# Moving the high and the low weight tiles to other places modulo 256 bytes in a one-core transformer kernel

## The chip, the cores and the metric

The kernel runs on one NeuronCore of a Trainium2 chip. The metric is the device time of one execution in microseconds (us), taken as the median of several runs. A difference of 0.2% (3.4 us) is about what a measurement of this kernel can tell from no change.

## The reference, cut to what matters

Two transformer layers follow each other on 512 tokens of width 1024, all in 32-bit floats:

```
h = LN(alpha*h + 0.5*swiglu(h))                  # ffn1, 1024 -> 2816 -> 1024
h = LN(alpha*h + mixers(h))                      # in 1024 -> 3072, out 1024 -> 1024
h = LN(alpha*h + cross_attention(h, mem))        # q, k, v, o: 1024 x 1024, 256 memory rows
h = LN(alpha*h + 0.5*swiglu(h))                  # ffn2
x = h + gate * (ga*(ya@w_a) + gb*(yb@w_b) + gc*(yc@w_c)) @ w_o
# ya: neighbourhood attention with 256 context keys, yb, yc: convolution branches; in 1024 -> 8704
```

Nearly all of the arithmetic is products of an activation matrix with a weight matrix. The change touches none of it: the same numbers are computed from the same operands.

## The kernel before, in words

**Splitting.** A 32-bit operand is split into a high part (rounded to the type fp32r, which TensorE multiplies in one pass) and a low part (what the rounding left, in fp32r as well). A product of two 32-bit matrices is then three matmuls: high weight by high activation, high weight by low activation, low weight by high activation. `product` does this (lines 417 to 423):

```
for n, (a, b) in enumerate(((wh, xh), (wh, xl), (wl, xh))):
    if moving_weights:
        a, b = b, a
    mm = nc.tensor.matmul(dst, a, b, start=start and n == 0, stop=stop and n == 2)
```

The first operand of `matmul` is the stationary one: it is loaded into the array by an LDWEIGHTS of its own, which the trace shows on the row PEld. The second, the moving one, is streamed past it. In most stages the weights are stationary, a piece of 128x128 (512 bytes in each partition), and an activation chunk of 512 tokens moves (2048 bytes in each partition; 256 tokens where the memory, the context or half of the tokens are meant). In token_strip (line 473), and in it only, the roles are exchanged: 512 columns of weights move and 128 tokens stand.

**The weight stream.** All the weights come from HBM as strips of 128x1024. SP loads each strip into one of four slots of `raw` (load, line 2201) once DVE has finished with the slot's last strip. ScalarE copies it to `w_hi` (split_hi, line 401, the instruction on line 407), VectorE writes raw minus w_hi to `w_lo` (split_lo, line 409, the instruction on line 414), and TensorE uses both (feature_strip, line 425, and its variants; the matmul itself is on line 422). ScalarE waits, before it writes a slot of w_hi, until TensorE is through with the strip that was there. Each of the three tiles has four slots.

**Stages.** ffn1 (to about 370 us, with its down projection), the token mixers (to 560), the output projection of the mixers and cross attention (to 780; the keys of the context, with ctx_hi and ctx_lo as moving tiles, near 762 to 774), ffn2 (to 1175), the neighbourhood attention and convolutions (to 1462), the merge and last projection (to 1707). The order within a stage is written out by hand on each engine, with semaphores between them.

**Where the tiles lie.** Tiles in SBUF are laid one behind the other in the order of their declaration, each rounded up to a multiple of 32 bytes, and a tile of an inner scope takes the place of those of a scope that was closed. These are the lines that matter:

```
172  raw = sb("raw", [P, RING, SB * P])            # 4 x 1024 x 4 = 16384 bytes in a partition
173  w_hi = sb("w_hi", [P, RING, SB * P], F32R)    # 16384
174  w_lo = sb("w_lo", [P, RING, SB * P], F32R)    # 16384
175  h = sb("h", [P, KD, T])                       # 16384
179  a_hi = sb("a_hi", [P, KD, T], F32R)           # 16384, a_lo the same
181  cols = sb("cols", [P, NCOLS])                 # 271 x 4 = 1084, rounded up to 1088
182  consts = sb("consts", [P, 2, P])
239  xs = sb("xs", [P, 3, 8, 2], F32, ph)          # 192
240  ctx_hi = sb("ctx_hi", [P, KD, M], F32R, ph)   # 8192, ctx_lo the same
```

Call the address of raw modulo 256 bytes r (it is 128). Since 16384 is a multiple of 256, w_hi, w_lo, h, a_hi and a_lo all begin at r too. The small tiles between a_lo and work add up to a multiple of 256, so hid_hi, hid_lo, mix_h, mix_l, side_hi, side_lo, y_hi, y_lo, m_hi, m_lo, memv_hi and xpt_hi, all the other operands of line 422, begin at r as well. Pieces within a tile are multiples of 512 bytes apart. Two kinds of tile stand elsewhere: consts and the constant matrices behind it begin at r + 64, since cols ends 64 bytes past a multiple of 256; ctx_hi and ctx_lo begin at r - 64, since xs ahead of them has 192 bytes.

Of the kernel before, what the change touches and what calls it, by code (L numbers as in the profile page):

```python
# [27 lines left out]
P = 128  # L28
# [129 lines left out]
def hybrid_blocks(nc, stream, ada_in, cond_in, x_in, mem_in, ctx_in, cols_in, const_in, mask_in, rows_in, wst_in, band_in, rpb_in,  # L158
                  out):
    with ExitStack() as ctx:  # L160
# [3 lines left out]
        def sb(name, shape, dt=F32, scope=ctx):  # L164
            return scope.enter_context(nc.sbuf_tensor(name, shape, dt))
# [4 lines left out]


        raw = sb("raw", [P, RING, SB * P])
        w_hi = sb("w_hi", [P, RING, SB * P], F32R)
        w_lo = sb("w_lo", [P, RING, SB * P], F32R)
        h = sb("h", [P, KD, T])
        with ExitStack() as ph:
            cond_row = sb("cond_row", [P, 2, D], F32, ph)
# [2568 lines left out]
```

## Time and profile before

| | us |
|---|---|
| median of 3 runs (1707.86 to 1708.67) | 1708.23 |
| span of the profiled execution, first to last instruction | 1706.6 |
| PE (matmuls) busy in it | 1691.5 |
| PEld (weight loads) busy | 1394.7 |
| DVE (VectorE) busy | 994.7 |
| ACT (ScalarE) busy | 683.6 |

The span is the only time that is recorded of the profiled execution; the median is 1.6 us above it. Busy times of different engines overlap. A matmul's recorded duration goes from its start to the end of its last result, so that successive matmuls overlap in the record; the pace of TensorE is read from the difference of two starts. The granted TensorE clock is 1.00 of full speed (2.4 GHz) in every stretch.

### The profile page before, as it was taken

How to read it: one execution, taken by the hardware profiler on the slowest of the kernel's cores; microseconds unless marked ns; L12 is line 12 of the kernel's file. 1: busy time of each engine (PE TensorE's matmuls, PEld its weight loads, DVE VectorE, ACT ScalarE, POOL GpSimd, SP SyncE). 2: the span in 40 equal slices, each digit the busy share in tenths (PEclk: the TensorE clock that was granted, in tenths of full speed). 3: DMA queues.
4: the chain of work that ended last, by engine and by line, in shares of the span. 5: the costliest groups of instructions: out<-in, count | busy, mean ns of one | idle time of the engine just before them, and what ended most of it. 6: DMA issues, size and time to landing. Idle time of an engine off the chain costs nothing.

```text
span 1706.6 us, 22901 instructions
## 1 busy us (share of the span) xinstructions
PE 1691.5 (99%) x8500; PEld 1394.7 (82%) x8500; DVE 994.7 (58%) x1341; ACT 683.6 (40%) x975; POOL 166.8 (10%) x158
## 2 busy tenths in 40 slices
PE   9999999999999999999999999999999999999999
PEld 7888888888787888888888888877778787788887
DVE  5333339987965784666333333457976869844442
ACT  4222232246454465434222223346454445732330
POOL 0000000112004521013000000013011020000000
DMA  5333247633122353223332233323333222243331
GB/s 216 98 98 98 91 138 231 222 121 119 52 98 66 109 182 137 67 82 123 98 98 94 92 130 117 109 87 118 85 99 95 86 83 86 74 123 109 104 109 62
DMA packets 51476, 188.05 MB, mean 110 GB/s; under 512 B 5776, under 2 KB 6288, under 8 KB 50512
## 3 DMA queue, kind: packets, MB, share of 16 engines
q1 hardware_dynamic: 44640, 161.50, 29.7%
q10 hardware_dynamic: 5184, 16.00, 2.9%
q0 software_dynamic: 1584, 9.60, 1.6%
q8 instruction: 47, 0.77, 0.2%
q14 instruction: 21, 0.17, 0.0%
HBM read 182.89 MB, written 4.19 MB: 110 GB/s over the span
## 4 chain that ended last, share of the span: by engine, by line
PE 89%; DVE 7%; ACT 2%; issue 1%; DMA 0%; POOL 0%; SPq 0%; DVEq 0%; ACTq 0%; POOLq 0%
PE proj L422 83%; DVE w_lo L414 1%; PE aux L1859 1%; PE aux L1846 1%; PE aux L1619 1%; PE aux L1836 1%; DVE y L2016 0%; ACT w_hi L407 0%; DVE score L1221 0%; DVE qk L1264 0%; DVE md L1242 0%; PE aux L566 0%; DVE qk L1265 0%; PE aux L1839 0%; DVE md L1241 0%
## 5 line engine op out<-in xcount | busy, mean ns | idle before, releaser
L414 DVE TENSOR_TENSOR w_lo<-raw,w_hi 128x1024 fp32r<-128x1024 f32 x300 | 380.5, 1270 | 388.8 <-ACT w_hi L407 382.0
L422 PE MATMUL proj<-a_hi,w_hi 128*128 128x512 f32 (+1 forms) x1536 | 600.8, 391 | 3.3 <-DVE a_lo L909 1.8
L422 PE MATMUL proj<-a_hi,w_lo 128*128 128x512 f32 (+1 forms) x1536 | 591.3, 385 | 0.0
L422 PE MATMUL proj<-a_lo,w_hi 128*128 128x512 f32 (+1 forms) x1536 | 591.0, 385 | 0.0
L407 ACT ACTIVATE w_hi<-raw 128x1024 fp32r<-128x1024 f32 x300 | 315.3, 1053 | 233.4 <-PE proj L422 164.3
L422 PEld LDWEIGHTS proj<-a_hi,w_hi 128*128 128x128 f32 x1536 | 288.5, 188 | 67.9 <-issue 5.8
L422 PEld LDWEIGHTS proj<-a_lo,w_hi 128*128 128x128 f32 x1536 | 288.7, 188 | 58.4 <-issue 2.9
L422 PEld LDWEIGHTS proj<-a_hi,w_lo 128*128 128x128 f32 x1536 | 288.5, 188 | 58.5
L422 PE MATMUL proj<-hid_hi,w_hi 128*128 128x512 f32 (+1 forms) x374 | 142.6, 381 | 0.0
L422 PE MATMUL proj<-hid_hi,w_lo 128*128 128x512 f32 (+1 forms) x374 | 140.9, 377 | 0.0
L422 PE MATMUL proj<-hid_lo,w_hi 128*128 128x512 f32 (+1 forms) x374 | 140.8, 377 | 0.0
L971 ACT ACTIVATE hid_hi<-work 128x512 f32 (+1 forms) x44 | 27.8, 632 | 196.5 <-DVE work L988 196.5
L988 DVE TENSOR_TENSOR work<-sq,proj 128x512 f32<-128x512 f32 x44 | 30.2, 687 | 106.7 <-PE proj L422 106.7
L2016 DVE SCALAR_TENSOR_TENSOR y<-glu,wtap,y 128x512 f32 (+1 forms) x120 | 90.6, 755 | 3.2
L422 PEld LDWEIGHTS proj<-hid_hi,w_hi 128*128 128x128 f32 x374 | 70.4, 188 | 13.9 <-issue 0.7
L422 PEld LDWEIGHTS proj<-hid_lo,w_hi 128*128 128x128 f32 x374 | 70.4, 188 | 13.6 <-issue 0.7
L422 PEld LDWEIGHTS proj<-hid_hi,w_lo 128*128 128x128 f32 x374 | 70.4, 188 | 12.9
L966 ACT ACTIVATE sq<-proj 128x512 f32<-128x512 f32 x44 | 26.3, 597 | 114.9 <-PE proj L422 114.9
L993 DVE TENSOR_TENSOR hid_lo<-work,hid_hi 128x512 f32 (+1 forms) x44 | 30.5, 693 | 39.7 <-ACT hid_hi L971 39.7
L728 POOL TENSOR_SCALAR h<-h,cols 128x512 f32<-128x512 f32 x32 | 40.7, 1275 | 98.2 <-DVE a_lo L710 50.6
L1906 ACT ACTIVATE npr<-aux,ns 128x512 f32<-128x512 f32 x32 | 22.0, 689 | 48.0 <-DVE ns L2031 48.0
L580 POOL TENSOR_TENSOR work<-h 128x512 f32<-128x512 f32 x3 | 4.7, 1574 | 364.2 <-DVE h L646 364.2
(368 smaller groups left out, 2011.1 us busy)
## 6 DMA issues: line engine op xcount, KB each, us to landing
raw<-stream SPq DMA_DIRECT2D x303, 512.0 KB, 3.5
ctxk<-ada_in ACTq DMA_DIRECT2D x12, 512.0 KB, 3.7
ctxv<-ada_in ACTq DMA_DIRECT2D x12, 512.0 KB, 3.9
out<-h ACTq DMA_DIRECT2D x7, 256.0 KB, 2.0
h<-x_in SPq DMA_DIRECT2D x3, 512.0 KB, 8.7
btab<-rpb_in POOLq DMA_DIRECT2D x4, 384.0 KB, 3.5
cond_row<-cond_in ACTq DMA_DIRECT2D x1, 1024.0 KB, 5.9
side<-mem_in POOLq DMA_DIRECT2D x1, 1024.0 KB, 5.2
```

Source lines behind the costliest of these rows:

```text
L407: nc.scalar.activation(w_hi[:, st.slot], raw[:, st.slot], ACT.Copy).then_inc(hi_ready, 1)
L414: nc.vector.tensor_tensor(w_lo[:, st.slot], raw[:, st.slot], w_hi[:, st.slot].bitcast(F32), ALU.subtract).then_inc(lo_ready, 1)
L422: mm = nc.tensor.matmul(dst, a, b, start=start and n == 0, stop=stop and n == 2)
L728: nc.gpsimd.tensor_scalar(m.dst[:, c], m.dst[:, c], 1.0, m.shift(c), ALU.mult, ALU.add).then_inc(n_raw, 1)
L966: nc.scalar.activation(sq[:, j // 2], res, ACT.Silu).then_inc(proj_read[g.slot], 1)
L971: nc.scalar.activation(hc, work[:, j // 2], ACT.Copy).then_inc(hid_h, 1)
L988: nc.vector.tensor_tensor(work[:, j // 2], sq[:, j // 2], res, ALU.mult).then_inc(proj_read[g.slot], 1)
L993: nc.vector.tensor_tensor(a, work[:, j // 2], b.bitcast(F32), ALU.subtract).then_inc(hid_l, 1)
L1619: mm = nc.tensor.matmul(aux[:, u % 2, t * M:(t + 1) * M], xq[:, 2 * hd + kk, at:at + P], memk[:, 2 * hd + kk], start=(kk == 0), stop=(kk = ...
L1836: nc.tensor.matmul(aux[:, n, :M], nq[part, at], grid(nk[part], ROWS, BAND_AT[cb], BAND), start=True, stop=True)
L1906: nc.scalar.activation(npr[:, u % 2], aux[:, u % 2], ACT.Exp, bias=ns[:, 0, u:u + 1], accum_out=ns[:, 1, u:u + 1]).then_inc(u_exp, 1)
L2016: ins = nc.vector.scalar_tensor_tensor(dst, src, wtap[:, tap:tap + 1], dst, ALU.mult, ALU.add)
```

## The change

Three unused tiles are declared between the others. w_hi moves up by 64 bytes, w_lo by 128, and h and everything behind it by 64 + 64 + 128 = 256 bytes.

```
         raw = sb("raw", [P, RING, SB * P])
+        sb("shift_hi", [P, 16])
         w_hi = sb("w_hi", [P, RING, SB * P], F32R)
+        sb("shift_lo", [P, 16])
         w_lo = sb("w_lo", [P, RING, SB * P], F32R)
+        sb("shift_behind", [P, 32])
         h = sb("h", [P, KD, T])
```

Modulo 256 bytes raw stays at r, w_hi comes to r + 64, w_lo to r + 128, and every other tile keeps its place: the activations at r, consts at r + 64, ctx_hi and ctx_lo at r - 64. No instruction, semaphore, DMA or order changes.

## Rows read from the trace of the kernel before

**Rows 1.** The page: span, busy time by engine, chain that ended last by engine and line.
```profile
span 1706.6 us, 22901 instructions
...
PE 1691.5 (99%) x8500; PEld 1394.7 (82%) x8500; DVE 994.7 (58%) x1341; ACT 683.6 (40%) x975; POOL 166.8 (10%) x158
...
PE 89%; DVE 7%; ACT 2%; issue 1%; DMA 0%; POOL 0%; SPq 0%; DVEq 0%; ACTq 0%; POOLq 0%
PE proj L422 83%; DVE w_lo L414 1%; PE aux L1859 1%; PE aux L1846 1%; PE aux L1619 1%; PE aux L1836 1%; DVE y L2016 0%; ACT w_hi L407 0%; DVE score L1221 0%; DVE qk L1264 0%; DVE md L1242 0%; PE aux L566 0%; DVE qk L1265 0%; PE aux L1839 0%; DVE md L1241 0%
```

**Rows 2.** Chain that ended last, by line, of 0:370, 370:560, 560:780, 780:1175, 1175:1462, 1462:1707 us.
```profile
by line: PE proj L422 96.6%; DMA h<-x_in 1.0%; PE aux L594 0.2%; DVE h L903 0.2%; DVE h L885 0.2%; DVE a_lo L2413 0.2%; ACT a_hi L2269 0.2%; PE aux L836 0.2%; issue 0.1%; ACT work L347 0.1%; PE aux L840 0.1%; DVE work L891 0.1%; DVE h L869 
...
by line: PE proj L422 55.4%; issue 4.6%; DVE score L1221 4.0%; DVE qk L1264 3.9%; DVE md L1242 3.6%; DVE qk L1265 3.6%; DVE md L1241 3.2%; ACT md L1269 3.0%; ACT md L1370 2.5%; PE aux L1313 1.9%; PE aux L1330 1.9%; PE aux L1322 1.8%; PE aux
...
by line: PE proj L422 59.6%; DVE w_lo L414 6.0%; PE aux L1619 4.7%; issue 2.9%; ACT w_hi L407 2.4%; DVE side L704 2.4%; DVE h L675 2.0%; DVE h L704 1.8%; DVE h L652 1.6%; DVE work L745 1.5%; DVE side_lo L710 1.4%; POOL work L736 1.4%; ACT x
...
by line: PE proj L422 95.4%; PE aux L566 1.7%; PE aux L1780 0.4%; issue 0.4%; DVE a_lo L710 0.3%; ACT L1917 0.3%; DVE w_lo L414 0.3%; PE aux L594 0.2%; PE aux L600 0.2%; PE aux L602 0.2%; PE aux L606 0.2%; PE aux L608 0.2%; DVE h L704 0.2%;
...
by line: PE proj L422 71.2%; PE aux L1859 5.7%; PE aux L1846 5.6%; PE aux L1836 3.3%; DVE y L2016 2.8%; PE aux L1839 2.3%; issue 1.6%; PE aux L1884 0.9%; PE aux L1874 0.9%; PE proj L1879 0.9%; DVE w_lo L414 0.9%; ACT L1917 0.4%; ACT L1932 0
...
by line: PE proj L422 98.0%; PE aux L546 0.4%; PE aux L562 0.4%; issue 0.2%; DVE h L2546 0.2%
```

**Rows 3.** Timeline of PE, 512-column matmuls: start us, duration us, what.
```profile
1501.00 0.39 PE L422 MATMUL proj<-a_lo,w_hi 128*128 128x512 f32 x1
1501.23 0.39 PE L422 MATMUL proj<-a_hi,w_lo 128*128 128x512 f32 x1
1501.45 0.39 PE L422 MATMUL proj<-a_hi,w_hi 128*128 128x512 f32 x1
...
1503.72 0.39 PE L422 MATMUL proj<-a_lo,w_hi 128*128 128x512 f32 x1
```

**Rows 4.** The same, 256 columns, moving tile side_hi or side_lo.
```profile
609.90 0.28 PE L422 MATMUL proj<-side_lo,w_hi 128*128 128x256 f32 x1
610.02 0.28 PE L422 MATMUL proj<-side_hi,w_lo 128*128 128x256 f32 x1
610.14 0.28 PE L422 MATMUL proj<-side_hi,w_hi 128*128 128x256 f32 x1
...
610.98 0.28 PE L422 MATMUL proj<-side_lo,w_hi 128*128 128x256 f32 x1
```

**Rows 5.** The same, 256 columns, moving tile ctx_hi or ctx_lo.
```profile
763.51 0.28 PE L422 MATMUL proj<-ctx_hi,w_hi 128*128 128x256 f32 x1
763.62 0.28 PE L422 MATMUL proj<-ctx_lo,w_hi 128*128 128x256 f32 x1
763.73 0.28 PE L422 MATMUL proj<-ctx_hi,w_lo 128*128 128x256 f32 x1
...
765.55 0.28 PE L422 MATMUL proj<-ctx_hi,w_hi 128*128 128x256 f32 x1
```

**Rows 6.** Instructions on tile side_hi: count, duration ns min/median/max, first and last start.
```profile
L422 PEld LDWEIGHTS proj<-side_hi,w_lo x64: 187/192/192, 588.9 to 617.1; 128*128 128x128 f32 x64
L422 PE MATMUL proj<-side_hi,w_lo x64: 277/283/283, 589.0 to 617.2; 128*128 128x256 f32 x64
L717 ACT ACTIVATE side_hi<-side,cols x8: 508/510/512, 582.0 to 592.9; 128x256 fp32r<-128x256 f32 x8
L710 DVE SCALAR_TENSOR_TENSOR side_lo<-side,cols,side_hi x8: 474/478/1508, 583.4 to 593.5; 128x256 fp32r<-128x256 f32 x8
```

**Rows 7.** The same for tile ctx_hi.
```profile
L422 PEld LDWEIGHTS proj<-ctx_hi,w_lo x32: 187/188/189, 762.9 to 773.5; 128*128 128x128 f32 x32
L422 PE MATMUL proj<-ctx_hi,w_lo x32: 276/276/281, 763.0 to 773.6; 128*128 128x256 f32 x32
L717 ACT ACTIVATE ctx_hi<-side,modv x8: 496/500/512, 658.2 to 673.3; 128x256 fp32r<-128x256 f32 x8
L710 DVE SCALAR_TENSOR_TENSOR ctx_lo<-side,modv,ctx_hi x8: 477/482/485, 658.7 to 673.9; 128x256 fp32r<-128x256 f32 x8
```

**Rows 8.** All of line 422: busy time and count, PE then PEld.
```profile
0.00:1707.00 1707.00, 1572.47 (x7146) 1287.11 (x7146) 1.00 0.34 110
```

**Rows 9.** Groups of line 422 with 256 columns, shapes kept apart.
```profile
L422 PE MATMUL proj<-side_hi,w_lo 128*128 128x256 f32 x64 | 18.1, 283 | 0.0
L422 PE MATMUL proj<-a_hi,w_lo 128*128 128x256 f32 x64 | 18.1, 283 | 0.0
L422 PE MATMUL proj<-hid_hi,w_lo 128*128 128x256 f32 x44 | 12.4, 283 | 0.0
```

**Rows 10.** The page: the two split instructions, ACT's and DVE's.
```profile
L414 DVE TENSOR_TENSOR w_lo<-raw,w_hi 128x1024 fp32r<-128x1024 f32 x300 | 380.5, 1270 | 388.8 <-ACT w_hi L407 382.0
L407 ACT ACTIVATE w_hi<-raw 128x1024 fp32r<-128x1024 f32 x300 | 315.3, 1053 | 233.4 <-PE proj L422 164.3
```

**Rows 11.** Instructions on tiles mv and xp, 128 columns.
```profile
L1313 PE MATMUL aux<-score,mv x32: 270/275/275, 502.8 to 508.7; 128*128 128x128 f32 x32
...
L1629 PE MATMUL aux<-consts,xp x32: 270/273/330, 686.6 to 711.7; 128*128 128x128 f32 x32
```

**Rows 12.** The page: DMA issues of the weight stream.
```profile
raw<-stream SPq DMA_DIRECT2D x303, 512.0 KB, 3.5
```

**Rows 13.** Busy us and counts in two stretches: PE, PEld, DVE, ACT, POOL; clock, DMA, GB/s.
```profile
1200.00:1300.00 100.00, 99.95 (x554) 79.33 (x553) 86.40 (x137) 50.35 (x87) 9.79 (x9) 1.00 0.27 85
1500.00:1600.00 100.00, 100.00 (x443) 82.81 (x442) 41.53 (x45) 30.32 (x38) 0.00 (x0) 1.00 0.35 111
```

More of the change, by code:

```diff
@@ L172, in hybrid_blocks @@
         raw = sb("raw", [P, RING, SB * P])
+        sb("shift_hi", [P, 16])
         w_hi = sb("w_hi", [P, RING, SB * P], F32R)
+        sb("shift_lo", [P, 16])
         w_lo = sb("w_lo", [P, RING, SB * P], F32R)
+        sb("shift_behind", [P, 32])
         h = sb("h", [P, KD, T])
```

## Prediction

> **What bounds the kernel now.** I read the page first. PE is busy for 1691.5 of the span's 1706.6 us, DVE for 994.7 and ACT for 683.6, and the chain that ended last runs for 83% of the span over one line of PE, 422, the matmul of `product` [rows 1]. Where that share lies comes from the same chain cut by stages [rows 2]: line 422 has 96.6% of ffn1's 370 us (357), 55.4% of the mixers' 190 (105), 59.6% of the next 220 (131), 95.4% of ffn2's 395 (377), 71.2% of the neighbourhood stage's 287 (204), 98.0% of the last 245 (240). That is 1415 us. A change that is only about places can gain or lose there, and only through the time from one matmul to the next.
>
> So the timeline of PE comes next. With 512 columns, 12 starts take 2.72 us, 226.7 ns each [rows 3]. At the granted clock of 1.00, 2.4 GHz [rows 8], 512 columns are 213.3 ns: each matmul costs 13.3 ns beyond its columns. With 256 columns and side_hi or side_lo moving, 9 starts take 1.08 us, 120.0 ns [rows 4], against 106.7 for the columns: 13.3 ns again. It is a charge per matmul, not per column.
>
> With ctx_hi or ctx_lo moving it is another: 18 starts take 2.04 us, 113.3 ns [rows 5], a charge of 6.7. The instruction, line, column count, clock and stationary tiles w_hi and w_lo are the same. The recorded durations agree: 276 instead of 283 ns for the matmul, 188 instead of 192 for the weight load [rows 6, 7]. What differs is where the moving tile begins: side_hi at r, like w_hi and w_lo, and ctx_hi at r - 64. The likely reason is that the load of the next weights and the stream of the running matmul start together and disturb each other when both start at the same place modulo 256 bytes.
>
> **The change part by part.** It adds and removes no instruction; three things move.
>
> *w_hi to r + 64.* The moving activations stay at r, so w_hi stands 64 bytes above them. That is just what rows 5 show (w at r, ctx at r - 64). Two of the three matmuls of a product have w_hi as stationary operand. I take 6.7 ns off each, 226.7 to 220.0. The bounds: 0, if the distance is not what matters, and the whole 13.3.
>
> *w_lo to r + 128.* The third matmul has its stationary operand 128 bytes above the moving one. No row shows this distance. It could save nothing (if places 128 apart count as the same), 6.7 (if only the same place is charged) or 13.3 (if the charge falls with the distance). I take 6.7: the nearest row, at 64, stands exactly halfway, and "not the same place" is the simplest reading of it. Both ends go into the range.
>
> *token_strip.* Here weights move and activations stand, so the sign is reversed. Nearest is a pair of plain 128-column matmuls: both operands at r, 275 ns; moving at r + 64 over stationary at r, 273 [rows 11]. The second is a transpose, so that is weak, but it points the same way. These strips are some 340 of 7146 matmuls; I treat them like the others.
>
> *The sum.* 6.7 of 226.7 ns is 2.94%, and 2.94% of 1415 us is 41.6. The matmuls of 256 columns (three groups each of 64, 64 and 44, and 144 more with the half strips and attention values [rows 9]) save 6.7 of 120, some 3 ns each more than 2.94% gives: 2 us. Together 43.6. All of line 422 has 7146 matmuls [rows 8]; those off the chain gain nothing. In the three mixed stages 441 us of the chain are line 422's and would give 13; DVE is busy for 86 of 100 us there against 42 in the last stage [rows 13], and its strings of work alternate with PE's in the chain. A faster PE meets them earlier and waits. I take a quarter of the 13 as lost, 3 us. That leaves 40.
>
> *The split instructions.* ACT's copy reads raw at r and writes r + 64, DVE reads r and r + 64 and writes r + 128. In the rows nearest to it, ACT took 500 ns with its output 64 away and 510 at the same place, DVE 482 and 478 [rows 6, 7]: 2% down, 1% up. Of DVE's 1270 ns [rows 10] 1% is 13 ns, and that line has 1% of the chain, 17 us: 0.2 us. I book nothing. The cover is PE's strip of 24 matmuls, 5.28 us after the change, over 1.05 of ACT and 1.27 of DVE; without it DVE's part would be 300 x 13 ns, 4 us.
>
> *The weight stream.* A strip of 512 KB would be asked for every 5.28 us instead of 5.44, 99 GB/s instead of 96, and lands in 3.5 us [rows 12] with four slots. Nothing. All else moves by 256 bytes and keeps its place.
>
> The profiled execution would have a span of 1706.6 - 40 = 1666.6; with the 1.6 us by which the median stands above it, **1668.2, say 1668 us**.
>
> By the Trainium skill ("TensorE: Matmul & The Clock Gate", Back-to-back issue gap) an isolated warm matmul of 512 columns follows the last after 512/2.4 + 2.5, about 216 ns, so 10.9 ns could go at most; were that reached everywhere, my estimate from the page would be 68 us less, near 1640. No row of line 422 shows that pace, and my sum does without it.
>
> **The rivals.**
>
> *w_lo gains nothing* (0.15). If places 128 apart collide like equal ones, only two thirds of the matmuls gain: 27 us, 1681. For it: rows show one distance only, and cannot exclude a period of 128. Against: nothing but simplicity.
>
> *w_lo, or all, gains more* (0.10). If w_lo's whole charge goes, 6242 / 3 matmuls of the chain (1415 us / 226.7 ns is 6242) save 6.7 ns more: 14 us, 1654. For: half a charge still stands at 64 bytes.
>
> *No change* (0.12): 1708. The place of the moving tile by itself, not its distance from the stationary one, could make the 113.3 ns: ctx_hi is the only moving operand of line 422 that begins elsewhere than r, and the change leaves the moving tiles at r. For: the rows can't part the two. Against: a single stream has little reason to run faster from r - 64, and the weight load, another stream, got shorter as well [rows 6, 7]. That the change doesn't do what it says (unused tiles given no room) belongs here, 0.01. Another way to the same time is two reads that cannot disturb each other at all, with the 6.7 ns due to something else near 763 us; against it are 18 even steps. I give it 0.02 of the 0.12. It is the rule of the Trainium skill ("SBUF — State Buffer", Who interferes with whom): PE has two read ports, one for the stream and one for the weight load, and never waits on anyone. By that rule the change does nothing; rows 4 and 5 speak against it, 120.0 against 113.3 ns.
>
> *Slower* (0.05). Half of the 256 bytes could be the worst distance, so that each w_lo matmul is charged more. The two w_hi matmuls give back 13.3 ns per product, so it decides from 13.3 ns more per w_lo matmul, 240 ns from start to start. At 20 ns more a product loses 6.7 ns, 6242 / 3 of them 14 us: 1722. For: no row excludes it. Against: the largest effect of place that a row shows is 6.7 ns.
>
> **How the numbers follow.** My forecast, 6.7 ns off nearly all, has 0.50, with 1661 to 1675 as its own range (all of the quarter lost in the mixed stages and more, or none of it and the products beside the chain). Mixed outcomes between 1675 and 1690, with the token strips or the mixed stages giving nothing back, have 0.08. With the rivals at 0.15, 0.10, 0.12 and 0.05 that is 1. The range reaches from 1652 (w_lo free of charge) to 1688 (w_lo without gain, and a third of the rest lost): 1 in 5 is left out above and below. Faster by over 0.2% (3.4 us): 0.83; the same: 0.12; slower: 0.05.
>
> **What the changed profile would show.** Starts 220.0 ns apart in rows 3's stretch and 113.3 in rows 4's; 188 for side_hi's weight load. If only w_hi gains, the steps read 220, 220, 227 in turn, the long one where w_lo is loaded during the matmul of a_lo. ctx's steps tell too: w_hi is then 128 above ctx_hi, w_lo 192 above it. PE's count in 1500 to 1600 us should rise from 443 [rows 13] to about 456. DVE's share of the chain should rise a little in the mixed stages. Steps still at 226.7 make the prediction wrong at its root; steps of 220 with a gain well under 40 us make the chain's share wrong.

## The result and the profile after

The changed kernel takes **1731.65 us** (median of 4 runs, 1731.64 to 1731.70), the kernel before 1708.08 (4 runs, 1707.86 to 1708.67): the ratio is 1.0137, with a 95% interval of 1.0122 to 1.0152. The forecast was 1668 in a range of 1652 to 1688. Sign and size are both wrong. The profiled execution's span went from 1706.6 to 1730.0 us, by 23.4. Every line of the changed file is 3 lower down, so line 422 is now 425, 414 is 417 and 407 is 410.

The page of the kernel after; its last columns are busy us and mean ns of one:

```profile
span 1730.0 us, 22901 instructions
...
PE 1716.2 (99%) x8500; PEld 1396.1 (81%) x8500; DVE 995.0 (58%) x1341; ACT 684.1 (40%) x975; POOL 165.9 (10%) x158
...
PEclk9999999999999999999999999999999999999999
...
PE 91%; DVE 6%; ACT 2%; issue 1%; DMA 0%; POOL 0%; SPq 0%; DVEq 0%; ACTq 0%; POOLq 0%
...
L417 DVE TENSOR_TENSOR w_lo<-raw,w_hi 128x1024 fp32r<-128x1024 f32 x300 | 380.1, 1268 | 401.6 <-ACT w_hi L410 394.9
...
L410 ACT ACTIVATE w_hi<-raw 128x1024 fp32r<-128x1024 f32 x300 | 315.6, 1054 | 239.8 <-PE proj L425 174.6
```

Beside [rows 1] PE is busy for 24.7 us more, with as many instructions; DVE, ACT and POOL stay within a microsecond, the clock is full in every slice, and the chain's share of PE rose from 89% to 91%. The two splits take 1268 and 1054 ns, against 1270 and 1053 [rows 10]. No other engine does more, and no new wait stands in the chain: the time went into PE's matmuls themselves.

The timeline of PE, kernel after (start us, duration us, what): first 256 columns with side moving, then 256 columns with ctx moving, then 512 columns:

```profile
618.12 0.28 PE L425 MATMUL proj<-side_hi,w_lo 128*128 128x256 f32 x1
618.24 0.28 PE L425 MATMUL proj<-side_hi,w_hi 128*128 128x256 f32 x1
618.36 0.28 PE L425 MATMUL proj<-side_lo,w_hi 128*128 128x256 f32 x1
...
619.19 0.28 PE L425 MATMUL proj<-side_hi,w_lo 128*128 128x256 f32 x1
...
774.98 0.28 PE L425 MATMUL proj<-ctx_hi,w_hi 128*128 128x256 f32 x1
775.10 0.28 PE L425 MATMUL proj<-ctx_lo,w_hi 128*128 128x256 f32 x1
...
777.14 0.28 PE L425 MATMUL proj<-ctx_hi,w_hi 128*128 128x256 f32 x1
...
1505.62 0.39 PE L425 MATMUL proj<-y_hi,w_lo 128*128 128x512 f32 x1
1505.85 0.39 PE L425 MATMUL proj<-y_hi,w_hi 128*128 128x512 f32 x1
1506.08 0.39 PE L425 MATMUL proj<-y_lo,w_hi 128*128 128x512 f32 x1
1506.31 0.39 PE L425 MATMUL proj<-y_hi,w_lo 128*128 128x512 f32 x1
1506.54 0.40 PE L425 MATMUL proj<-y_hi,w_hi 128*128 128x512 f32 x1
...
1507.70 0.39 PE L425 MATMUL proj<-y_hi,w_lo 128*128 128x512 f32 x1
```

With side, 9 starts take 1.07 us: 119 ns each, a little less than the 120.0 of [rows 4]. With ctx, 18 starts take 2.16 us: 120.0 ns where [rows 5] show 113.3. With 512 columns, 9 starts (three products) take 2.08 us: 231 ns each where [rows 3] show 226.7. Over all products of the last stage the mean steps are 235.8 ns (while a_hi or y_hi runs against w_hi), 228.3 (the low moving part against w_hi) and 229.2 (against w_lo): 693.3 ns per product against 680.0. **A product of 512 columns costs 13.3 ns more**, where 20 less was forecast.

The same in the groups by shape of the kernel after (busy us, mean ns), whose mean before was 390, 389 and 389 for the three:

```profile
L425 PE MATMUL proj<-y_hi,w_hi 128*128 128x512 f32 x96 | 38.3, 399 | 0.3 <-issue 0.3
L425 PE MATMUL proj<-y_hi,w_lo 128*128 128x512 f32 x96 | 37.6, 392 | 0.0
L425 PE MATMUL proj<-y_lo,w_hi 128*128 128x512 f32 x96 | 37.4, 390 | 0.0
```

And busy us and counts in two stretches of the kernel after (PE, PEld, DVE, ACT, POOL; clock, DMA, GB/s):

```profile
1200.00:1300.00 100.00, 100.00 (x519) 78.70 (x518) 86.95 (x129) 49.39 (x84) 8.37 (x9) 1.00 0.32 94
1500.00:1600.00 100.00, 99.71 (x432) 80.81 (x431) 46.53 (x53) 35.01 (x48) 0.00 (x0) 1.00 0.36 111
```

PE starts 432 matmuls in 1500 to 1600 us where it started 443 [rows 13]: 2.5% fewer, though its load unit is busy for less time than before. It is slower from start to start, and not because the loads take longer: 187 ns each, before and after.

**Does this account for the whole?** 1415 us of the chain [rows 2] at 680.0 ns are 2081 products; at 13.3 ns each they give 27.7 us, against 23.4 in the span. By stages, from the same instruction in both traces: side_hi's first matmul comes 7.5 us later (588.8 to 596.3 us), ctx_hi's first 9.3 (762.4 to 771.7), ffn2's last one on hid_hi 16.2 (1136.2 to 1152.4), y_hi's first 19.5 (1479.6 to 1499.1), y_hi's last 22.8 (1659.2 to 1682.0). From y_hi's first to its last, 179.6 us of unbroken products, the rule gives 3.5 us and the traces 3.3. What is missing of the 27.7 is in the mixed stages, which have 2 us less before ctx_hi than the rule gives, and 1.8 less in the neighbourhood stage. Part of it is the rule's own fault: it counts the 756 matmuls of 256 columns on line 422, some 90 us, as if they lost like the others. They gained or lost little (side's mean step went from 119.8 to 118.2 ns, ctx's from 113.6 to 119.9), so up to 1.8 of the 4.3 us are no loss that was absorbed; that is an estimate, since not all of them are on the chain.

### The profile page after: what moved, and what is told of

It reads as the page before. It is cut to its first block, busy times and chain, and to the rows that moved or that the text cites. A ratio compares the mean times of both kernels' runs of the same rounds, so it can differ in the third digit from the quotient of the medians.

```text
span 1730.0 us, 22901 instructions
## 1 busy us (share of the span) xinstructions
PE 1716.2 (99%) x8500; PEld 1396.1 (81%) x8500; DVE 995.0 (58%) x1341; ACT 684.1 (40%) x975; POOL 165.9 (10%) x158
## 4 chain that ended last, share of the span: by engine, by line
PE 91%; DVE 6%; ACT 2%; issue 1%; DMA 0%; POOL 0%; SPq 0%; DVEq 0%; ACTq 0%; POOLq 0%
PE proj L425 85%; DVE w_lo L417 1%; PE aux L1862 1%; PE aux L1849 1%; PE aux L1622 1%; PE aux L1839 1%; DVE score L1224 0%; DVE qk L1267 0%; DVE md L1245 0%; PE aux L1842 0%; PE aux L569 0%; DVE qk L1268 0%; ACT w_hi L410 0%; DVE md L1244 0%; ACT md L1272 0%
## 5 line engine op out<-in xcount | busy, mean ns | idle before, releaser
L425 PE MATMUL proj<-a_hi,w_hi 128*128 128x512 f32 (+1 forms) x1536 | 612.9, 399 | 2.9 <-DVE a_lo L912 1.8
L417 DVE TENSOR_TENSOR w_lo<-raw,w_hi 128x1024 fp32r<-128x1024 f32 x300 | 380.1, 1268 | 401.6 <-ACT w_hi L410 394.9
L410 ACT ACTIVATE w_hi<-raw 128x1024 fp32r<-128x1024 f32 x300 | 315.6, 1054 | 239.8 <-PE proj L425 174.6
L969 ACT ACTIVATE sq<-proj 128x512 f32<-128x512 f32 x44 | 26.3, 597 | 119.1 <-PE proj L425 119.1
L2166 ACT ACTIVATE gate<-proj 128x512 f32<-128x512 f32 x24 | 14.3, 596 | 66.8 <-PE proj L425 66.8
```

Of the source, the lines that this page charges most:

```text
L410: nc.scalar.activation(w_hi[:, st.slot], raw[:, st.slot], ACT.Copy).then_inc(hi_ready, 1)
L417: nc.vector.tensor_tensor(w_lo[:, st.slot], raw[:, st.slot], w_hi[:, st.slot].bitcast(F32), ALU.subtract).then_inc(lo_ready, 1)
L969: nc.scalar.activation(sq[:, j // 2], res, ACT.Silu).then_inc(proj_read[g.slot], 1)
```

## Experiments

In what follows a distance is the start of the stationary tile less the start of the moving one, modulo 256 bytes: w_hi and w_lo stand at 0 and 0 before, at 64 and 128 after. A step is the time from one matmul's start to the next's. A rhythm is a pattern of steps that repeats; a row can take some matmuls to settle into it. Seven variants of the kernel change only empty tiles; four small kernels time matmuls of TensorE alone. Diffs of variants are against the kernel after, unless the text says otherwise. The kernel before ran beside each group of them, at 1707.7 to 1708.5 us. Each variant but e_side192 ran once, so that a difference of 2 us between two of them says nothing by itself.

### e_map: the step at each distance

A kernel that holds stationary tiles at 16 places 32 bytes apart, and some finer ones, runs twelve equal matmuls in a row for each:

```
one = lambda d: s[d][:]
run([one(0)], [x_hi], 512, 30)
for n in (512, 256):
    for d in SPOTS:
        run([one(d)], [x_hi], n, 12)
...
for n in (512, 256):
    for a in COARSE:
        for b in COARSE:
            run([one(a), one(a), one(b)], [x_hi, x_lo, x_hi], n, 6)
```

> This kernel leaves the whole computation out: TensorE alone runs fp32r matmuls, each behind a weight load of its own, with the stationary 128x128 tile (named s000 to s480) so many bytes above the place of the moving tile modulo 512, 12 in a row for each distance, with 512 and with 256 columns, then rows of three (a, a, b) as in a product. The theory that a distance has one charge, whatever the column count (the prediction's): about 13.3 ns over the columns at distance 0 and about 6.7 at 64 with both column counts. The theory that the charge depends on when, within the stream, the load meets it: 256 columns repeat 120.0 at 0, 113.3 at 64 and 120.0 at 128, and 512 columns give another curve, above 226.7 at 64. The theory that it is the change between two distances that costs: each distance alone costs no more than 226.7 with 512 columns, and only the rows of three with a other than b go above it, to 236. The theory of the moving tile's own place: x64 over s000 and over s064 read alike, below x_hi.

Mean step of the last eight of each row, ns:

| distance | 0 | 32 | 64 | 96 | 128 | 160 | 192 | 224 |
|---|---|---|---|---|---|---|---|---|
| 512 columns | 226.6 | 233.4 | 233.2 | 234.6 | 232.1 | 233.6 | 228.5 | 233.2 |
| 256 columns | 119.1 | 118.4 | 117.9 | 117.1 | 120.0 | 119.8 | 117.8 | 118.0 |

With 512 columns, distance 0, the one that the change gives up, is the fastest of all. Places between these (16, 48, 80) give 233.5, 233.4 and 232.0. From 256 on the table repeats to within 0.2 ns at 512 columns. With the moving tile 64 bytes higher the same distances give the same steps (0: 226 to 227 once settled, 32: 233.4, 64: 233.2, 96: 234.6, 128: 232.1), but for 192, which gave 233.2 there and 228.6 one period on: the first sign that a distance can have two paces. With 256 columns the order is another, and everything lies within 3 ns.

Timeline of PE in this kernel: equal matmuls stand in one line, start us, us from the first's start to the last's end, and the number. Ten matmuls are nine steps and one own duration (the step and 163 ns). The first four have 512 columns at distance 0, 64, 128 and 192, the last two 256 columns at 64 and at 576, which is 64 modulo 256:

```profile
19.24 4.04 PE L232 MATMUL proj<-x_hi,s 128*128 128x512 f32 x17
...
25.45 2.50 PE L232 MATMUL proj<-x_hi,s 128*128 128x512 f32 x10
...
31.05 2.48 PE L232 MATMUL proj<-x_hi,s 128*128 128x512 f32 x10
...
36.64 2.45 PE L232 MATMUL proj<-x_hi,s 128*128 128x512 f32 x10
...
122.87 1.34 PE L232 MATMUL proj<-x_hi,s 128*128 128x256 f32 x10
...
142.79 1.31 PE L232 MATMUL proj<-x_hi,s 128*128 128x256 f32 x10
```

The first is (4.04 - 0.39) / 16 = 228 ns with its settling; the second (2.50 - 0.40) / 9 = 233; the last (1.31 - 0.277) / 9 = 115, settling at 113.3 to 114. So one and the same distance gave 118 ns in one row and 114 in another, which e_cols takes up.

In rows of three, as `product` runs them (w_hi's distance, w_lo's distance), a product of 512 columns takes 682.5 ns at (0, 0), with its settling, 693.2 at (64, 0), 697.8 at (0, 128), 700.0 at (64, 64), and 693.2 at (64, 128). The last is the changed kernel's 693.3, and (64, 64) is that of e_both64 below; (0, 128) is 4 ns above what e_lo128 shows. No pair was faster than (0, 0); the slowest was (192, 128) at 702.8. These are means of the last four products of six. The change's loss is there without a DMA, without DVE or ACT at work, and without any wait.

### e_both64, e_hi64, e_lo128: the change's parts

The prediction's nearest row said that 64 bytes save 6.7 ns. Both tiles at distance 64:

```
         sb("shift_hi", [P, 16])
         w_hi = sb("w_hi", [P, RING, SB * P], F32R)
-        sb("shift_lo", [P, 16])
         w_lo = sb("w_lo", [P, RING, SB * P], F32R)
-        sb("shift_behind", [P, 32])
+        sb("shift_behind", [P, 48])
```

> Both weight tiles 64 bytes above the activations, so that every load of a product has the same distance. If only the change between two distances costs, 512 columns go 220.0 ns from start to start, as the prediction had it, and the time is about 1668 us. If distance 64 itself is worse than 0 with 512 columns, steps are 229 to 236 ns and the time is 1722 to 1766 us. 256 columns should repeat the 113.3 ns of the context's matmuls in either case.

Measured: **1744.23 us**, span 1742.6, slower than the change. Only w_hi moved:

```
-        sb("shift_lo", [P, 16])
+        sb("shift_lo", [P, 48])
         w_lo = sb("w_lo", [P, RING, SB * P], F32R)
-        sb("shift_behind", [P, 32])
```

> Only w_hi is moved, by 64 bytes; w_lo stays at the activations' place. If each load is charged by its own distance, the loads of w_hi keep the 236 and 229 ns of the changed kernel and that of w_lo goes back to 226.7: 691.7 a product instead of 680, some 24 us, 1732 us. If the change between distances costs, it is about that too (there still are two). If the 128 bytes of w_lo are what costs, the time falls below 1708, to about 1681.

Measured: **1739.0 us**, span 1737.4. Only w_lo moved, to distance 128:

```
-        sb("shift_hi", [P, 16])
         w_hi = sb("w_hi", [P, RING, SB * P], F32R)
-        sb("shift_lo", [P, 16])
+        sb("shift_lo", [P, 32])
```

> Only w_lo is moved, by 128 bytes. If each load is charged by its own distance, only the load of w_lo takes its 228.3 ns and the others 226.7: some 3 us more, 1711 us. If the change between distances costs, the three steps are uneven and the time is near 1731 us. If w_lo's distance is what costs in the changed kernel, it is all there: 1731 us or more.

Measured: **1733.04 us**, span 1731.4. Groups by shape in e_both64, e_hi64 and e_lo128:

```profile
L424 PE MATMUL proj<-y_hi,w_hi 128*128 128x512 f32 x96 | 38.0, 396 | 0.2 <-issue 0.2
L424 PE MATMUL proj<-y_hi,w_lo 128*128 128x512 f32 x96 | 38.0, 395 | 0.0
L424 PE MATMUL proj<-y_lo,w_hi 128*128 128x512 f32 x96 | 38.0, 395 | 0.0
```

```profile
L424 PE MATMUL proj<-y_lo,w_hi 128*128 128x512 f32 x96 | 38.1, 397 | 0.0
L424 PE MATMUL proj<-y_hi,w_lo 128*128 128x512 f32 x96 | 37.8, 394 | 0.0
L424 PE MATMUL proj<-y_hi,w_hi 128*128 128x512 f32 x96 | 37.3, 389 | 0.3 <-issue 0.3
```

```profile
L424 PE MATMUL proj<-y_hi,w_lo 128*128 128x512 f32 x96 | 38.1, 397 | 0.0
L424 PE MATMUL proj<-y_lo,w_hi 128*128 128x512 f32 x96 | 38.0, 396 | 0.0
L424 PE MATMUL proj<-y_hi,w_hi 128*128 128x512 f32 x96 | 37.4, 390 | 0.3 <-issue 0.3
```

In e_both64 all three stand at 395 to 396, with steps of 233.3 ns and 700.0 per product. In these groups of the other two, one of the three keeps the old duration and the other two are longer: the long ones are the two after which the stationary distance changes, and the one behind which w_hi is loaded again stays as it was. In the changed kernel just that one is the longest (399).

y_hi runs in the last stage only. There a product takes 693.5 ns in e_hi64, 693.4 in e_lo128 and 693.4 in the changed kernel. So **the parts don't add up**: each move alone costs 13.3 ns per product, and the two together cost 13.3 and not 26.7. Where then do the further 6 to 7 us of e_hi64 come from? From its first 1050 us. In its ffn1 and in ffn2 up to there a product takes 700.0 ns, with none of the three steps as before (means 234.4, 231.0 and 234.6). At 1050.1 us a short product of plain fp32 (`aux<-sq,consts`) cuts into the row, and behind it the same products on the same tiles take 693.3 (226, 236, 232). Three windows of 100 us of unbroken products in e_hi64, two with 430 starts and the last with 434; e_lo128 has 434 to 435 in all three:

```profile
100.00:200.00 100.00, 100.00 (x430) 80.35 (x429) 33.73 (x36) 28.13 (x36) 0.00 (x0) 1.00 0.31 94
900.00:1000.00 100.00, 100.00 (x430) 80.32 (x430) 34.48 (x36) 28.19 (x36) 0.00 (x0) 1.00 0.30 93
1520.00:1620.00 100.00, 100.00 (x434) 81.28 (x433) 43.02 (x47) 30.62 (x38) 0.00 (x0) 1.00 0.35 111
```

So with 512 columns, too, one arrangement can run in two rhythms. The 1.4 us between e_lo128 and the change are within the noise.

In e_both64 side_hi stands where ctx_hi stood in [rows 5], 64 below the weights. Its matmuls (duration ns min, median, max) now take the 276 of [rows 7]:

```profile
L424 PE MATMUL proj<-side_hi,w_lo x64: 276/276/415, 599.8 to 628.7; 128*128 128x256 f32 x64
```

So the distance was the cause of rows 5, as the prediction read them, and the same kernel at the same distance is 6.7 ns slower per matmul with 512 columns.

### e_cols: from 256 to 512 columns

> This kernel leaves the whole computation out, like e_map: matmuls alone, 16 in a row for 256, 320, 384, 448 and 512 columns at distances 0, 64, 128 and 192, then the same rows again, each behind six different short rows of other matmuls. The prediction read the surplus of 13.3 ns at distance 0 as a charge per matmul: then 320 columns take 146.7, 384 take 173.3, 448 take 200.0 ns at distance 0. The new theory reads it as a charge per column, one sixteenth (226.7 and 113.3 are both 17/16 of the columns' own time), with the disturbance by the load on top of it: then no row is below 141.7, 170.0, 198.3 ns, and 512 columns at distance 0 stand at their floor and can't gain from any place. If what a distance costs depends on how a row began, the six repetitions differ: 256 columns at 64 read 113.3 in some and 118 in others; if it does not, all six read 117.9, 512 columns at 0 read 226.7 and 512 at 64 read 233.

Rows of 16 equal matmuls with 256, 320, 384, 448 and 512 columns at four distances. Mean of the last nine steps, ns:

| columns | 256 | 320 | 384 | 448 | 512 |
|---|---|---|---|---|---|
| the columns' own time | 106.7 | 133.3 | 160.0 | 186.7 | 213.3 |
| distance 0 | 120.0 | 146.7 | 173.3 | 202.7 | 228.0, once settled 226.7 |
| distance 64 | 117.8 | 146.7 | 176.8 | 202.2 | 233.6 |
| distance 128 | 119.0 | 146.8 | 176.1 | 203.4 | 231.7 |
| distance 192 | 117.8 | 146.7 | 173.3 | 200.0 | 228.9 |

Over the columns' own time, distance 0 costs 13.3 ns per matmul at 256, 320, 384 and 512 columns and 16.0 at 448. Distance 64 costs 11.1, 13.3, 16.8, 15.6 and 20.3. So the order of the two turns round on the way, though not evenly: at 256 columns 64 is the better, at 320 they are equal, at 384 0 is by 3.4 ns, at 448 they are within 0.5 (and 192 is the fastest), at 512 0 is by 7.

The second half of this kernel puts other matmuls ahead of the row. Timeline of PE (start us, us, number), distance 0 with 256, 384 and 512 columns, and then three rows of 256 columns at distance 64, each behind another predecessor:

```profile
20.30 1.84 PE L232 MATMUL proj<-x_hi,s 128*128 128x256 f32 x14
...
37.38 2.62 PE L232 MATMUL proj<-x_hi,s 128*128 128x384 f32 x14
...
61.67 3.37 PE L232 MATMUL proj<-x_hi,s 128*128 128x512 f32 x14
...
92.50 1.75 PE L232 MATMUL proj<-x_hi,s 128*128 128x256 f32 x14
...
94.93 1.81 PE L232 MATMUL proj<-x_hi,s 128*128 128x256 f32 x14
...
105.28 1.75 PE L232 MATMUL proj<-x_hi,s 128*128 128x256 f32 x14
```

Fourteen matmuls are 13 steps and one duration: (1.84 - 0.28) / 13 = 120.0; of the last three, (1.75 - 0.276) / 13 = 113.4 and (1.81 - 0.281) / 13 = 117.6. **At distance 64 a row of 256 columns locks into one of two rhythms**, 113.3 ns in three of six histories and 117.8 in the other three, and keeps it for as long as the row lasts. Distance 0 always gave 120.0 once settled, and 192 always 117.8. With 512 columns distance 0 always settled to 226.7 and 64 to 233.0 or more; 192 gave 228.9 five times and 233.3 once. The 113.3 ns from which the prediction took its price was the faster of two rhythms of a short matmul.

### e_moving64, e_all64, e_behind256: is it the distance?

The weights stay at r and everything behind them moves up by 64 (distance 192; against the kernel before):

```
         w_lo = sb("w_lo", [P, RING, SB * P], F32R)
+        sb("shift_behind", [P, 16])
         h = sb("h", [P, KD, T])
```

> The weights stay and h and everything behind it, all activations among it, move by 64 bytes, so that every stationary weight tile is 64 below the moving one (192 above it). If the distance decides and not a tile's own place, the step is that of distance 192 in the map, 228.5 to 233.3 ns, and the time 1720 to 1749 us. If the place of the weight tiles decides, nothing changes, 1708 us. The context's tiles come to the weights' place: 119 to 120 instead of 113.3 ns.

Measured: **1721.62 us**, span 1720.0. Steps of 226 to 232 ns, about 229 in the mean, the 228.5 of the map's single rows at distance 192; the map's rows of three at (192, 192) took the other pace, 233.3. Everything moves by 64, raw and weights too (against the kernel before):

```
+        sb("shift_all", [P, 16])
         raw = sb("raw", [P, RING, SB * P])
```

> All tiles move by 64 bytes, raw too: every place changes and no distance does. If the distance decides, 1708 us and 226.7 and 113.3 ns as before. If a place by itself decides, another time, by 10 us or more.

Measured: **1708.48 us**, span 1706.8. All behind the weights moves by 256 (against the kernel before):

```
         w_lo = sb("w_lo", [P, RING, SB * P], F32R)
+        sb("shift_behind", [P, 64])
```

> Of the change only that h and everything behind it moves up by 256 bytes; both weight tiles stay with raw. The map has the period 256, so nothing should change: 1708 us, 226.7, 120.0 and 113.3 ns. If the distance counts modulo 512 or more, this is a distance of 256 and the steps differ from 226.7.

Measured: **1708.52 us**, span 1706.8. Groups by shape in e_all64, then in e_behind256, at the kernel before's 390 ns:

```profile
L423 PE MATMUL proj<-y_hi,w_hi 128*128 128x512 f32 x96 | 37.4, 390 | 0.5 <-issue 0.5
```

```profile
L423 PE MATMUL proj<-y_hi,w_hi 128*128 128x512 f32 x96 | 37.4, 390 | 0.5 <-issue 0.5
```

Every tile 64 bytes higher changes nothing; all behind the weights 64 higher costs 13 us; 256 higher costs nothing. What decides is the distance between the two operands of TensorE, with a period of 256 bytes.

### e_side192: can the short matmuls gain?

Only side_hi and side_lo move, to r - 64, where ctx stands (against the kernel before). Then x_hi with 512 columns keeps distance 0, and side gets ctx's place:

```
             side = sb("side", [P, KD, M], F32, ph)
+            sb("shift_side", [P, 48], F32, ph)
             side_hi = sb("side_hi", [P, KD, M], F32R, ph)
             side_lo = sb("side_lo", [P, KD, M], F32R, ph)
+            sb("shift_back", [P, 16], F32, ph)
```

> Only side_hi and side_lo move, to r - 64, where ctx_hi and ctx_lo stand: the weights are 64 above them. All matmuls of 512 columns keep distance 0, but 96 of token_strip. If the disturbance by the load is what 256 columns pay at distance 0 (6.7 ns of the 120.0), the 192 matmuls with side moving fall to 113.3 to 118, 0.4 to 1.3 us in all, and the time is 1707 to 1708 us, at most 0.1% off. If the prediction's reading had been right also for 512 columns, it would be the same here: this run tests the only part of it that e_both64 bore out.

Measured: 1709.04 us (10 runs, 1707.65 to 1711.44) against 1708.51 (13 runs, 1707.55 to 1709.29), ratio 1.0004 with an interval of 0.9995 to 1.0014: no difference. The 256-column matmuls lock in at 118 ns, not 113.3 (281 against 276 in duration), which is 2 ns each on 192 of them, 0.4 us; the token strips, which have side as stationary tile against 512 columns of weights, go from 227 to some 231 ns and give it back. No version was faster than the kernel before.

### e_load and e_cross: load against stream?

The prediction took the next load of weights and the running stream to collide. If so, a load of fewer columns should be charged less:

```
for n in (512, 256):
    for w in (128, 96, 64, 32):
        for d in COARSE:
            for k in range(16):
                nc.tensor.matmul(proj[:w, 0, :n], s[d][:, :w], x_hi[:, :n], start=True, stop=True)
```

> This kernel leaves the whole computation out: matmuls alone, 16 in a row at distances 0, 64, 128 and 192, with 128, 96, 64 and 32 stationary columns, under 512 and under 256 moving columns; then plain fp32 operands, 8 in a row. If the charge over the columns' own time comes from the weight load and the stream disturbing each other, it falls with the length of the load: 13.3 ns and 20 ns with 128 stationary columns, about half with 64, a few ns and no difference between the distances with 32. If it is a fixed cost of each matmul that a distance only modifies, it stays near 13 ns for all lengths. Plain fp32: the profile of before shows 428 to 429 ns for 512 columns, 2 ns over the columns' own two passes, so distances should differ by 1 or 2 ns at most.

Time over the columns' own (213.3 or 106.7 ns), at distances 0, 64, 128, 192:

| stationary columns | with 512 columns moving | with 256 columns moving |
|---|---|---|
| 128 | 13.3, 20.3, 18.3, 15.7 | 13.7, 11.1, 12.3, 11.1 |
| 96 | 16.7, 14.8, 18.1, 19.6 | 9.8, 10.1, 12.3, 11.1 |
| 64 | 15.6, 19.3, 17.8, 14.8 | 6.7, 6.7, 10.1, 6.7 |
| 32 | 18.4, 18.4, 16.9, 18.6 | 6.7, 6.7, 6.7, 6.7 |

The loads did get shorter: 188, 161, 134 and 108 ns in the record, and each starts 2 to 5 ns behind the start of the running matmul. With 256 columns moving the charge falls with the load's length, and with 32 stationary columns the distance no longer counts: as the theory has it. With 512 the charge doesn't fall. The distances come close to each other only with 32 stationary columns, at 16.9 to 18.6 ns. Timeline of PE in e_load, distance 0: 128 and then 32 stationary columns against 512, then the same against 256:

```profile
20.31 3.33 PE L244 MATMUL proj<-x_hi,s 128*128 128x512 f32 x14
...
64.58 3.40 PE L244 MATMUL proj<-x_hi,s 128*32 128x512 f32 x14
...
79.16 1.84 PE L244 MATMUL proj<-x_hi,s 128*128 128x256 f32 x14
...
101.55 1.75 PE L244 MATMUL proj<-x_hi,s 128*32 128x256 f32 x14
```

A quarter of the load makes the 512-column row slower ((3.33 - 0.39) / 13 = 226, then (3.40 - 0.395) / 13 = 231). Groups of plain fp32 matmuls in the same kernel: each counts twice, two records for one instruction, 429 ns per record with 512 columns and 216 with 256, at all four distances:

```profile
L248 PE MATMUL proj<-src,p 128*128 128x512 f32 x64 | 27.6, 592 | 0.0
...
L248 PE MATMUL proj<-src,p 128*128 128x256 f32 x64 | 14.0, 379 | 0.0
```

So of the two forms measured only fp32r shows the effect; why plain fp32 doesn't was not tested. e_cross then asks whether the distance of a matmul to its own weights counts, or that of the running stream to the next weights, by letting the two alternate in step and against each other:

```
run([one(0), one(64)], [x_hi, x64], n, 12)
run([one(64), one(0)], [x_hi, x64], n, 12)
```

> This kernel leaves the whole computation out: matmuls alone, 24 in a row. A weight load runs beside the stream of the matmul before its own, so two distances can be told apart: to the tile that moves beside the load (cross), and to the tile that moves over the loaded weights afterwards (own). Rows that alternate the places 0 and 64 of both operands: with stationary and moving in step the own distance is 0 and the cross distance 64; with them in counter-step the own one is 64 and the cross one 0. If load and running stream disturb each other, 512 columns read 226.7 ns in counter-step and 231 to 236 in step. If the own distance counts, it is the reverse. The prediction's mechanism (load against running stream) is the first. With PSUM banks taken in turn or with one long accumulation nothing changes in either case: 226.7 at distance 0 and 233 at 64; if the charge had to do with writing one bank again and again, it would fall with two banks.

With 512 columns: both operands fixed at the same place, 226.7 ns; in step (own distance 0, crossed 64 and 192), 231.7; in counter-step (own 64 and 192, crossed 0), 231.7; only the stationary tile alternating, 230.0; only the moving one, 229.8. Timeline of PE in e_cross, first 22 at distance 0, then 22 with the stationary tile alternating:

```profile
20.84 5.15 PE L232 MATMUL proj<-x_hi,s 128*128 128x512 f32 x22
...
42.87 5.22 PE L232 MATMUL proj<-x_hi,s 128*128 128x512 f32 x22
```

Were the crossed distance alone decisive, counter-step would run at 226.7, and were the own one, step would. Neither does. The same rows with 256 columns do take a side: 120.0 fixed, 116.7 in step, 120.0 in counter-step. Did the own distance decide, in step (own 0) would be at 120.0 and counter-step (own 64 and 192) near 118; it is the other way round. There the crossed distance decides, that of the running stream to the next weights, as the prediction's likely reason has it, as far as rows that ran once each can tell. Writing to two PSUM banks in turn, or into one accumulation, left all four distances as they were with 512 columns (226.7, 233.3, 231.7, 228.8 ns) and with 256: neither the bank nor the accumulation has a part in it. **What stays open** is whether it is the two reads that collide, and why 512 columns order the distances otherwise than 256. A row of matmuls without any load between them was not tried, nor a 16-bit type.

## Why the prediction was wrong

- *What bounds the kernel* [rows 1, 2]: right. The loss is on line 422, now 425, over the chain's share, and 2081 products at 13.3 ns make 27.7 us where 23.4 came. The same sum is as near in e_both64: 20.0 ns per product gives 41.6 us and 36.0 came.
- *A charge of 13.3 ns per matmul, not per column* [rows 3, 4]: right at distance 0, with 16.0 at 448 columns.
- *The distance between the operands decides*: right, by e_all64, e_behind256 and e_moving64. With it the rival "no change" fell, in its two main forms. One was the moving tile's own place. The other was the rule of the Trainium skill ("SBUF — State Buffer", Who interferes with whom), by which the two reads of PE are independent and it never waits on anyone. By that rule the change would do nothing; moving empty space alone took this kernel from 1708 to 1744 us.
- *The likely reason, the next load against the running stream, worst at the same place*: borne out with 256 columns, by e_load and by e_cross (120.0 in counter-step, 116.7 in step). With 512 columns the same place is the best one, counter-step ran at 231.7 where the reason asks for 226.7, and a shorter load took nothing off. What happens there stays open.
- **The step that failed**: "I take 6.7 ns off each, 226.7 to 220.0", for w_hi at r + 64. The price came from 256-column rows [rows 5] and was carried over to 512 columns, on the ground that the charge was per matmul. The charge at distance 0 is, and the one at distance 64 is not: 226.7 becomes 233.3 where both weights stand at 64. With w_hi alone there a product lost 13.3 to 20.0 ns, where 13.3 were to be gained. The bounds were given as 0 and 13.3 to the good; nothing excluded a loss, since no row showed 512 columns at any distance but 0. Even at 256 columns 113.3 ns was one rhythm of two.
- *w_lo at r + 128*: the same step; alone it costs 25 us, 13.3 ns per product. The rival "slower" had the right side and a wrong place: it put the loss on the w_lo matmul alone, at 240 ns or more, with w_hi's two giving back 6.7 each. The w_lo step is 229.2, the long one is 235.8 while the high part runs against w_hi, and none gives anything back.
- *The sum as separate terms* was wrong in itself. In the last stage each move alone costs 13.3 ns per product, and so do both together. And one arrangement can have two paces, 700.0 and 693.3 ns in e_hi64.
- *token_strip*, forecast like the others: the strips with side went from 227.1 to 231.2 ns in the mean (233.2 and 234.8 where w_hi moves, 225.7 where w_lo does), a loss of the same size as the others'.
- *256 columns*: side went from 119.8 to 118.2 ns where 113.3 was forecast; ctx from 113.6 to 119.9. The ctx matmuls lost just what the change was forecast to bring the others.
- *Mixed stages take part of it*: right in kind. As a quarter of a gain was to be lost there, some 2 to 4 of 27.7 us of loss were absorbed.
- *Splits and weight stream at nothing*: right. The splits take 1268 and 1054 ns, and DMA has 0% of the chain.
- The Trainium skill's 216 ns for an isolated warm matmul ("TensorE: Matmul & The Clock Gate", Back-to-back issue gap) was reached by no fp32r row at any of the distances measured; the lowest settled row is at 226.7. The plain fp32 rows, 429 ns for 2 times 213.3, are 2.4 ns over their columns, near the 2.5 ns of that page's formula.

## What to carry to other kernels

A duration read at one operand shape is no price for another: what 256-column rows saved, 512-column rows paid for. In these runs fp32r products with a fresh stationary tile for each matmul were fastest, at 512 columns, with both operands beginning at the same place modulo 256 bytes, so a tile put in ahead of one of them can cost 0.8 to 2% without touching an instruction. Where a change rests on a pace that only one stretch shows, a small kernel with rows of equal matmuls at each distance gives the table within one run. One row is not enough, though: the pace can depend on what ran before, so each should be repeated behind others.

## What the hardware showed that was not expected

- The pace of fp32r matmuls depends on the distance of their operands modulo 256 bytes: 226.7 ns at 0, 228.5 or 233.3 at 192, and 232 to 235 elsewhere, with 512 columns; 113.3 to 120.0 with 256.
- It has memory: 256 columns at distance 64 ran at 113.3 or 117.8 ns, by what came before, and the 512-column products of e_hi64 at 700.0 or 693.3 ns.
- Effects of two operands don't add: 13.3 ns per product in the last stage for w_hi alone, for w_lo alone and for both (1739.0, 1733.0 and 1731.7 us).
- At distance 0, a load of 32 instead of 128 columns made 512-column matmuls slower (226.7 to 231.8 ns) and 256-column ones faster (120.3 to 113.3).
